# Padding the narrow fp32 matmuls of a recurrent layer to the whole array, and an earlier place for its spreads

## The reference

```python
xx = jnp.pad(h, ((0, 0), (1, 0), (0, 0)))[:, :T] - h
xr, xw, xk, xv, xa, xg = (h + xx * mu[i] for i in range(6))
r = xr @ w_r
k = xk @ w_k
v = xv @ w_v
logw = -jax.nn.softplus(-(w0 + jnp.tanh(xw @ w1) @ w2)) - 0.5
a = jax.nn.sigmoid(a0 + (xa @ a1) @ a2)
g = jax.nn.sigmoid(xg @ g1) @ g2
kk = (k * k_k).astype(jnp.float32).reshape(B, T, H, N)
kk = kk / jnp.maximum(jnp.sqrt(jnp.sum(kk * kk, axis=-1, keepdims=True)), 1e-12)
k = k * (1.0 + (a - 1.0) * k_a)
...
m = jnp.mean(y, axis=-1, keepdims=True)
var = jnp.mean(jnp.square(y - m), axis=-1, keepdims=True)
y = ((y - m) * lax.rsqrt(var + GN_EPS)).reshape(B, T, D) * ln_g + ln_b
bonus = (jnp.sum(rh * kh * r_k, axis=-1, keepdims=True) * vh).reshape(B, T, D)
out = ((y + bonus) * g).astype(h.dtype) @ w_o
```

## Time and profile before

| | us |
|---|---|
| median of 3 runs | 2586.24 (2584.41 to 2588.34) |
| span of the profiled execution | 2583.7 |
| PE busy | 2498.8 (97%), 12240 instructions |
| DVE busy | 1161.4 (45%) |
| ACT busy | 937.5 (36%) |
| POOL busy | 1020.1 (39%) |
| mean granted clock of PE | 0.982 of full |

### The profile page before, as it was taken

How to read it: one execution, slowest core, us unless ns; L and a number is a source line. 1 busy time by engine, 2 the same in 40 slices (tenths; PEclk the granted TensorE clock), 3 DMA queues, 4 the chain that set the end, 5 groups by cost and what they waited for, 6 DMA issues and landing times.

```text
span 2583.7 us, 32306 instructions
## 1 busy us (share of the span) xinstructions
PE 2498.8 (97%) x12240; PEld 1938.1 (75%) x12240; DVE 1161.4 (45%) x1979; ACT 937.5 (36%) x1582; POOL 1020.1 (39%) x617
## 2 busy tenths in 40 slices
PE   7999999999989999999999999999999899999998
PEld 5776567888846668885787888888767687888887
DVE  5113654113152676643723365164389533562462
ACT  3545553222245462223443422123333534322222
POOL 4331545444522232212561545345424443445344
PEclk9999899999989999898999999999999999999999
DMA  3122013333411110002331233233222221333232
GB/s 129 58 66 87 17 33 89 95 96 96 126 49 49 57 58 2 2 1 77 110 117 50 82 98 107 89 97 98 82 66 85 87 90 58 90 97 108 88 94 69
DMA packets 55567, 196.99 MB, mean 76 GB/s; under 512 B 6701, under 2 KB 8877, under 8 KB 54733
## 3 DMA queue, kind: packets, MB, share of 16 engines
q1 hardware_dynamic: 54464, 192.44, 24.2%
q10 hardware_dynamic: 974, 2.80, 0.3%
HBM read 193.12 MB, written 2.10 MB: 76 GB/s over the span
## 4 chain that ended last, share of the span: by engine, by line
PE 46%; DVE 6%; ACT 1%; issue 0%; DVEq 0%; ACTq 0%
PE ps L364 11%; PE ps L366 11%; PE ps L365 11%; DVE ps L2993 4%; PE ps L439 3%; PE ps L440 3%; PE ps L441 3%; PE ps L2836 1%; PE ps L2859 1%; PE ps L3006 1%; DVE ps L3155 0%; PE ps L2604 0%; PE ps L2636 0%; PE ps L2609 0%; PE ps L2846 0%; PE ps L3050 0%
## 5 line engine op out<-in xcount | busy, mean ns | idle before, releaser
L463 POOL TENSOR_TENSOR w_lo<-raw,w_hi 128x1024 fp32r<-128x1024 f32 x342 | 819.6, 2407 | 1015.4 <-ACT w_hi L455 1015.1
L364 PE MATMUL ps<-ahead_hi,w_hi 128*128 128x512 f32 x1216 | 481.0, 396 | 2.0 <-issue 2.0
L366 PE MATMUL ps<-ahead_hi,w_lo 128*128 128x512 f32 x1216 | 473.3, 389 | 0.0
L365 PE MATMUL ps<-ahead_lo,w_hi 128*128 128x512 f32 x1216 | 473.1, 389 | 0.0
L455 ACT ACTIVATE w_hi<-raw 128x1024 fp32r<-128x1024 f32 x342 | 352.8, 1049 | 172.1 <-PE ps L441 91.1
L364 PEld LDWEIGHTS ps<-ahead_hi,w_hi 128*128 128x128 f32 x1216 | 228.3, 188 | 53.0 <-issue 6.4
L365 PEld LDWEIGHTS ps<-ahead_lo,w_hi 128*128 128x128 f32 x1216 | 228.3, 188 | 50.8 <-issue 4.1
L730 DVE TENSOR_TENSOR x_stream<-x_stream,ps 128x512 f32<-128x512 f32 x79 | 54.3, 688 | 468.4 <-PE ps L366 278.4
L366 PEld LDWEIGHTS ps<-ahead_hi,w_lo 128*128 128x128 f32 x1216 | 228.3, 188 | 47.8
L3127 ACT ACTIVATE ffn_s<-ps 128x512 f32<-128x512 f32 x44 | 26.4, 599 | 322.3 <-DVE ps L3155 322.3
L439 PE MATMUL ps<-ffn_a_hi,w_hi 128*128 128x512 f32 x342 | 133.5, 390 | 3.0 <-DVE ffn_a_lo L3160 2.9
(11 more groups left out here) (431 smaller groups left out, 4625.2 us busy)
## 6 DMA issues: line engine op xcount, KB each, us to landing
raw<-in_wall SPq DMA_DIRECT2D x346, 512.0 KB, 3.6
x_stream<-in_x SPq DMA_DIRECT2D x8, 256.0 KB, 7.5
cw<-in_cmp_w SPq DMA_DIRECT2D x1, 2048.0 KB, 7.9
out_y<-x_stream SPq DMA_DIRECT2D x16, 128.0 KB, 1.8
lora_a<-in_lora_a ACTq DMA_DIRECT2D x1, 1152.0 KB
dist<-in_consts SPq DMA_DIRECT2D x1, 1088.0 KB, 11.0
mem<-in_mem SPq DMA_DIRECT2D x1, 1024.0 KB, 5.9
gwb<-in_lora_b SPq DMA_DIRECT2D x1, 1024.0 KB
```

The lines of the kernel that those rows point to most:

```text
L364: pe.matmul(out, hi, src.hi[:, t, 0:width], start=first, stop=False)
L365: pe.matmul(out, hi, src.lo[:, t, 0:width], start=False, stop=False)
L366: return pe.matmul(out, lo, src.hi[:, t, 0:width], start=False, stop=last)
L463: e.tensor_tensor(self.w.lo[:, s, :], self.raw[:, s, :], as_float(self.w.hi[:, s, :]), ALU.subtract).then_inc(lo_r.sem, 1)
```

## The change

All of these matmuls get an operand of more than 64 rows or columns:

- `WIDE` is 66. Head sums, bonus sums and the variance take a slice of 66 columns from the constants (`k.own(m)`) in place of 16 columns of `picks`, and their result has 66 rows, of which the upper 50 are zero sums. The spreads (L1870, L2401, L2636) contract 66 rows; the added rows of the spread matrix are zero. ACT and DVE treat 66 rows where they treated 16 (roots, maximum, reciprocal, the copy of the bonus). `picks` and its transfer are gone from the recurrent layer.
- The low-rank inputs take all 128 columns from their first column on; the last part of the gate, 32 columns, now starts at column 160 and lands in rows 96 to 127. The rate matmul and the second gate matmul contract 128 rows; DVE clears the rows that they add, with two memsets, and ACT waits for these too.
- Transfers: `lora_b` 128 rows for 65, the spread matrix 66 rows for 16 (twice), the constants two columns more.

And the places: `middle` is called behind every step. The queries' spread of tile t-1 is issued behind step 1 of tile t, `cumulate(1)` stays behind step 3; spread(7) is issued behind step 1 of the values' tile 0. On DVE `key_normed` comes ahead of `bonus_in`.

```diff
--- before.py
+++ after.py
@@ -52,5 +52,6 @@
 HEAD_TILES = 10
-
-
-CONST_SIZES = [("ident", 128), ("blockones", 128), ("negtri", 128), ("m4", 512), ("cum", 129), ("own", 2 * HEAD_TILES - 2 + 64),
+WIDE = 66
+
+
+CONST_SIZES = [("ident", 128), ("blockones", 128), ("negtri", 128), ("m4", 512), ("cum", 129), ("own", 2 * HEAD_TILES - 2 + WIDE),
                ("fan_scale", 1), ("fan_bias", 1),
@@ -148,2 +149,7 @@
         return self.vecs[:, c:c + 1]
+
+    def own(self, m):
+
+        c = CST["own"] + 2 * HEAD_TILES - 2 - 2 * m
+        return self.consts[:, c:c + WIDE]
 
@@ -414,4 +420,4 @@
                             mm.then_inc(self.released.sem, 1)
-                        if self.middle is not None and q == 3:
-                            self.middle(pe, 4 * i + j)
+                        if self.middle is not None:
+                            self.middle(pe, 4 * i + j, q)
                     mm.then_inc(used.sem, 1)
@@ -1594,3 +1600,3 @@
 
-    PARTS = ((1, 5, 0, 64), (4, 6, 64, 64), (5, 7, 128, P), (5, 4, 256, 32))
+    PARTS = ((1, 5, 0), (4, 6, 64), (5, 7, 128), (5, 4, 160))
 
@@ -1613,3 +1619,3 @@
         pe.matmul(k.ps[:, 4, :], k.ones[:, :], k.squares[:, :], start=True, stop=True).then_inc(summed.sem, 1)
-        rec.wait(pe, "lora_loaded", 64)
+        rec.wait(pe, "lora_loaded", 48)
         for m in range(KD):
@@ -1618,5 +1624,5 @@
                 rec.wait(pe, "lora_mixed", t + 1)
-                for mu, bank, c, w in self.PARTS:
+                for mu, bank, c in self.PARTS:
                     if mu == i:
-                        mm = pe.matmul(k.ps[0:w, bank, :], rec.lora_a[:, m, c:c + w], rec.mixes[:, t % 6, :], start=(m == 0),
+                        mm = pe.matmul(k.ps[:, bank, :], rec.lora_a[:, m, c:c + P], rec.mixes[:, t % 6, :], start=(m == 0),
                                        stop=(m == KD - 1))
@@ -1629,3 +1635,3 @@
         act.activation(k.root[:, :], k.ps[:, 4, :], ACT.Sqrt, scale=1.0 / D, bias=k.bias[1e-6]).then_inc(root.sem, 1)
-        rec.wait(act, "constant_made", 3)
+        rec.wait(act, "constant_made", 5)
         for m in range(KD):
@@ -1645,3 +1651,3 @@
         rec.done(act.activation(rec.inner_g[:, 0, :], k.ps[:, 7, :], ACT.Sigmoid), "lora_inner")
-        rec.done(act.activation(rec.inner_g[0:32, 1, :], k.ps[0:32, 4, :], ACT.Sigmoid), "lora_inner")
+        rec.done(act.activation(rec.inner_g[96:P, 1, :], k.ps[96:P, 4, :], ACT.Sigmoid), "lora_inner")
 
@@ -1654,2 +1660,4 @@
         rec.done(v.memset(rec.inner_w[64:65, :], 1.0), "constant_made")
+        rec.done(v.memset(rec.inner_a[64:P, :], 0.0), "constant_made")
+        rec.done(v.memset(rec.inner_g[0:96, 1, :], 0.0), "constant_made")
         v.wait_ge(root.sem, root(1))
@@ -1697,3 +1705,2 @@
         self.sm, self.omka, self.keeps = s.tile("sm", KD, 12), s.tile("one_minus_ka", KD), s.tile("one_minus_mu", 48)
-        self.picks = s.tile("picks", 4 * HEAD_TILES - 2)
         s = at(151)
@@ -1731,3 +1738,3 @@
             "state_zeroed", "y_sums", "y_taken", "spread_loaded")}
-        k.advance(64, "lora_loaded")
+        k.advance(48, "lora_loaded")
         k.advance(KD, "spread")
@@ -1753,5 +1760,4 @@
 
-        for dst, src in ((self.lora_a[:, :, :], self.a["lora_a"]), (self.wb[0:65, :, :], self.a["lora_b"][0:65, 0:2, :]),
-                         (self.picks[:, :], self.a["consts"][:, CST["pick"]:CST["spread"]]),
-                         (self.spread[0:2 * KD, :], self.a["consts"][0:2 * KD, CST["spread"]:CST["spread"] + D])):
+        for dst, src in ((self.lora_a[:, :, :], self.a["lora_a"]), (self.wb[:, :, :], self.a["lora_b"][:, 0:2, :]),
+                         (self.spread[0:WIDE, :], self.a["consts"][0:WIDE, CST["spread"]:CST["spread"] + D])):
             self.done(e.dma_start(dst, src), "lora_loaded", 16)
@@ -1780,3 +1786,3 @@
         sp.wait_ge(self.v_used.sem, self.v_used(KD))
-        self.done(sp.dma_start(self.wide[0:2 * KD, :], self.a["consts"][0:2 * KD, CST["spread"]:CST["spread"] + D]),
+        self.done(sp.dma_start(self.wide[0:WIDE, :], self.a["consts"][0:WIDE, CST["spread"]:CST["spread"] + D]),
                   "spread_loaded", 16)
@@ -1808,5 +1814,4 @@
     def heads_sum(self, pe, m):
-        c = HEAD_TILES * 2 - 2 - 2 * m
         pe.wait_ge(self.k_free.sem, self.k_free(m + 1 + RING))
-        self.done(pe.matmul(self.k.ps[0:2 * KD, 7, :], self.picks[:, c:c + 2 * KD], self.sq[:, m % 2, :], start=(m == 0),
+        self.done(pe.matmul(self.k.ps[0:WIDE, 7, :], self.k.own(m), self.sq[:, m % 2, :], start=(m == 0),
                             stop=(m == KD - 1)), "heads_summed")
@@ -1819,3 +1824,3 @@
             wait(pe, "rates", t)
-        done(pe.matmul(k.ps[:, 4, :], self.wb[0:64, 1, t * P:(t + 1) * P], self.inner_a[0:64, :], start=True, stop=True),
+        done(pe.matmul(k.ps[:, 4, :], self.wb[:, 1, t * P:(t + 1) * P], self.inner_a[:, :], start=True, stop=True),
              "rate_sums")
@@ -1869,3 +1874,3 @@
             self.wait(pe, "kk_inverse", 2)
-        self.done(pe.matmul(self.k.ps[:, 6, :], self.spread[0:2 * KD, self.chunk(p)], self.rt[0:2 * KD, :], start=True,
+        self.done(pe.matmul(self.k.ps[:, 6, :], self.spread[0:WIDE, self.chunk(p)], self.rt[0:WIDE, :], start=True,
                             stop=True), "spread")
@@ -1874,12 +1879,11 @@
 
-        c = HEAD_TILES * 2 - 2 - 2 * p
         self.wait(pe, "bonus_in", p + 1)
-        self.done(pe.matmul(self.k.ps[0:2 * KD, 7, :], self.picks[:, c:c + 2 * KD], self.t0[:, :], start=(p == 0),
+        self.done(pe.matmul(self.k.ps[0:WIDE, 7, :], self.k.own(p), self.t0[:, :], start=(p == 0),
                             stop=(p == KD - 1)), "bonus_sums")
 
-    def queries_middle(self, pe, t):
-        if t == 1:
+    def queries_middle(self, pe, t, q):
+        if t and q == 1:
+            self.spread_tensor(pe, t - 1)
+        if t == 1 and q == 3:
             self.cumulate(pe, 1)
-        if t:
-            self.spread_tensor(pe, t - 1)
 
@@ -1919,3 +1923,3 @@
         k, wait, done = self.k, self.wait, self.done
-        t, rows = 4 * i + j, 2 * KD
+        t, rows = 4 * i + j, WIDE
         if t == 0:
@@ -1964,2 +1968,4 @@
         wait(v, "key_gained", p + 1)
+        wait(v, "spread", p + 1)
+        done(v.scalar_tensor_tensor(A_, A_, k.vec("k_k", p), k.ps[:, 6, :], ALU.mult, ALU.mult), "key_normed")
         if p:
@@ -1967,4 +1973,2 @@
         done(v.scalar_tensor_tensor(self.t0[:, :], r, k.vec("r_k", p), K_, ALU.mult, ALU.mult), "bonus_in")
-        wait(v, "spread", p + 1)
-        done(v.scalar_tensor_tensor(A_, A_, k.vec("k_k", p), k.ps[:, 6, :], ALU.mult, ALU.mult), "key_normed")
         wait(v, "grown", 2 * p + 2)
@@ -1979,5 +1983,7 @@
 
-    def values_middle(self, pe, t):
-        if t == 1:
+    def values_middle(self, pe, t, q):
+        if t == 0 and q == 1:
             self.spread_tensor(pe, KD - 1)
+        if q != 3:
+            return
         for p in ((), (2,), (), (5,), (7,), (), (), ())[t]:
@@ -2039,3 +2045,3 @@
                 wait(act, "bonus_sums", KD)
-                done(act.activation(self.bonus[0:2 * KD, :], k.ps[0:2 * KD, 7, :], ACT.Copy), "bonus_kept")
+                done(act.activation(self.bonus[0:WIDE, :], k.ps[0:WIDE, 7, :], ACT.Copy), "bonus_kept")
             self.gather(act, p)
@@ -2400,3 +2406,3 @@
         wait(pe, "spread_loaded", 16)
-        done(pe.matmul(k.ps[:, 3, :], self.wide[0:2 * KD, self.chunk(p)], self.bonus[0:2 * KD, :], start=True, stop=True),
+        done(pe.matmul(k.ps[:, 3, :], self.wide[0:WIDE, self.chunk(p)], self.bonus[0:WIDE, :], start=True, stop=True),
              "spread_sums")
@@ -2590,3 +2596,3 @@
         pe.matmul(k.ps[:, 5 + m % 3, :], self.wb[:, 0, m * P:(m + 1) * P], self.inner[:, 0, :], start=True, stop=False)
-        pe.matmul(k.ps[:, 5 + m % 3, :], self.wb[0:32, 1, m * P:(m + 1) * P], self.inner[0:32, 1, :], start=False, stop=True
+        pe.matmul(k.ps[:, 5 + m % 3, :], self.wb[:, 1, m * P:(m + 1) * P], self.inner[:, 1, :], start=False, stop=True
                   ).then_inc(go.sem, 1)
@@ -2594,3 +2600,3 @@
     def tensor(self, pe):
-        k, y, rows = self.k, self.y, 2 * KD
+        k, y, rows = self.k, self.y, WIDE
         me, ce, sq, va, rt, iv, sp_r, go, n1, n2, nd, zh, zl = self.marks
@@ -2607,4 +2613,3 @@
             pe.wait_ge(sq.sem, sq(m + 1))
-            c = CST["own"] + HEAD_TILES * 2 - 2 - 2 * m
-            pe.matmul(k.ps[0:rows, 2, :], k.consts[:, c:c + rows], self.sqt[:, m % 2, :], start=(m == 0),
+            pe.matmul(k.ps[0:rows, 2, :], k.own(m), self.sqt[:, m % 2, :], start=(m == 0),
                       stop=(m == KD - 1)).then_inc(va.sem, 1)
@@ -2625,3 +2630,3 @@
 
-        k, rows = self.k, 2 * KD
+        k, rows = self.k, WIDE
         iv, sp_r, n1 = self.marks[5], self.marks[6], self.marks[8]
@@ -3357,3 +3362,3 @@
     lora_b[0, 64] = n["rwkv_w0_2"][0]
-    lora_b[2], lora_b[3, :32] = n["rwkv_g2_2"][0][:P], n["rwkv_g2_2"][0][P:]
```

(3 more changed lines are left out.)

## The result

| | before | changed |
|---|---|---|
| median of 4 runs, us | 2585.32 (2576.16 to 2588.34) | 2568.09 (2565.78 to 2569.46) |
| ratio, 95% interval | | 0.9942 (0.9922 to 0.9962) |
| span of the profiled execution | 2583.7 | 2567.7 |
| mean granted clock of PE | 0.982 | 0.984 |
| PE busy | 2498.8 | 2474.2 |

The medians differ by 17 us (the ratio, which is taken run against run, says 10 to 20), the profiled spans by 16.0; 4 were forecast, and 2577.5 was the low end. The kernel is faster, by a way that the forecast had at nothing.

The account below looks back on a forecast made before the run. TensorE was taken as the bound in the keys and memory stages, DVE in the queries; -8.1 + 3.3 + 2.6 + 3.4 - 2.4 - 2.7 = -3.9 us took the median 2586.24 to 2582.3, range 2577.5 to 2586.0.

Parts of the forecast that it names:

- State loop: State loop: late spreads stand among 64 by 64 products, so a change of shape stays on both sides: 0.
- the rule that the prediction used: TensorE's clock falls back after idle gaps between matmul bursts; a sum without the rule would be 3.4 lower.
- The price of a fall: On the path: a slow stretch lasts 3.5 us at half clock, so one fall costs 1.7; two taken, +3.4.
- Cost of the moves: Queries' tile 1 loses 3.3 us, values' tiles 0 and 1 lose 2.6, two clock falls add 3.4.
- Inputs and keys: Low-rank inputs -3.5 us and keys -5.2: TensorE enters the queries 8.7 earlier, the first reciprocal comes 8.1 earlier.
- Queries' loop: Queries, tiles 2 to 7: DVE paces them, so padding only lengthens TensorE's wait and the early spread costs nothing: 0.
- GroupNorm: GroupNorm: TensorE's variance and mean pair shrinks from 2.02 to 1.72 us; -2.4 at the start of the memory stage.
- Memory stage: Second block's memory stage: gate and spread save a little under 0.39 us per tile over eight tiles; 2.7 kept.
- C: Rival, whole kernel: padding saves nothing and only the moves act, +10 us, 2596.3; chance 0.05.
- A: Rival, new stalls: one fall of the clock (-5.6 us, 2580.6) or none (-7.3, 2578.9); chance 0.33.
- B: Rival, queries and values: the moves help and neither stall costs, -13 us, 2573; chance 0.07.
- End of the program: Stretch behind the memory stage up to the program's end: no further shift forecast, 0.

Follow-up runs that it names:

- e7: All of the padding with spreads and DVE operations in their old places, but late spreads contract 64 rows instead of 66: 2558.6 us, ratio 0.9906.
- e3: All of the padding without the moves, spreads and the two DVE operations in their old places: 2553.9 us, ratio 0.9878 against the kernel before.
- e1: The changed kernel with only the state loop's late spreads put back to contracting 16 rows: 2579.2 us, ratio 0.9977 against the kernel before.
- e2: The kernel before with only the late spreads padded to 66 rows, and the bonus sums to 66 columns: 2571.3 us, ratio 0.9945.
- e6: The changed kernel with only the last spread put back in the values' tile 1, fourth step: 2560.2 us, ratio 0.9908 against the kernel before.
- e4: The kernel before with the new places and new DVE order alone, no padding: 2591.1 us, ratio 1.0022.
- e10: All padding, early spreads and new DVE order; first spread behind cumulate(1), last at the values' tile 1, second step: 2555.3 us, ratio 0.9895.
- e9: All of the padding with spreads and DVE operations in their old places, but late spreads contract 32 rows: 2557.1 us, ratio 0.9898.

## Why the prediction was wrong

- **State loop: 0. This is the step that failed.** It measured -14.3. The term was held at nothing for two reasons, and both fell. The products behind the late spread are of 64 by 64 in the first tile only; in the others the padding saves 0.19 each (1.4 up to the last tile, e7 against e3). And above all, the low clock of that stretch, 0.93 before, was taken as given. The falls there have no idle time in front of them, so the rule that the prediction used, falls behind stalls, did not see them. The Trainium skill, "TensorE: Matmul & The Clock Gate", "Why this matters for your kernels", advises against idle gaps between bursts. At the two stalls of the changed kernel these traces agree; that avoiding gaps is not enough to keep the clock up, the loop of the kernel before shows. The forecast missed by 13 us; e1 gives 11 of them back with eight narrow matmuls, and e2 has 9.6 in the loop from eight wide ones.
- **The price of a fall, 1.7, was too low as well.** It is half of a stretch of 3.4, but the stretches behind the two stalls were 6.8 long. The earlier trace rows had one of 13.6 behind a stall beside the one of 3.5 that was taken. How long it is differs between executions with the same stall: behind the first one, of 3.52 to 3.54, it was 6.8 in the changed kernel and 3.4 in e1 and e6, and behind the stall of 2.21 in e4 there was none. From the reciprocal to the queries' loop DVE lost 6.2, 5.0, 4.9 and 3.5 us in these four. The idle times themselves were right to half a microsecond.
- **Cost of the moves, 9.3 (3.3 + 2.6 + 3.4):** 14 by the medians, 13.2 at the start of the solve (e3). Up to the queries' loop the forecast of -3.1 and the measured -2.8 agree by luck, since two errors cancel: without the stall it is -9.6 (e3, from the end of the first block) where the prediction had -8.1, and the stall with its falls cost 6.9 where it had 5.0. In the values the move cost 6.3 where it had 4.3, and the solve came at +3.3 against the first block's end, where +1.2 was forecast. (The terms of the start of products(1) add up to 933.2 and not to 933.4, which changes nothing.)
- **Inputs and keys, -8.7:** right. The reciprocal, forecast at -8.1, starts 8.0 earlier, 9.0 against the first block's end. About 1 of it comes from the slow stretch in the low-rank inputs, 10.2 long where it was 13.7 before: in e6, where it is 13.7 again, the reciprocal is 7.8 earlier.
- **Queries' loop, 0:** right (e10).
- **GroupNorm, -2.4:** -0.8. The slow stretch of 10.2 (1201.6 before, 1193.1 after) reaches 1.6 us further into GroupNorm, since that starts 10 earlier and the stretch only 8.5. In e1, where it reaches as far as before, the gain is 1.6. So the stretch is half of the miss; the other half is open.
- **Memory stage, -2.7:** -2.95, right.
- **Rivals.** C, padding without effect, is out: in e3 the solve starts 9.9 earlier against the first block's end, and the whole is 31 us faster than before. The same page's "K=32 single mm = same time as K=128" holds for the matmul's own time (1.12 at 16 rows, 1.13 at 66), not for its neighbours, which start later at 16 rows, nor for the clock. C's other half, the moves alone, was priced at +10 and measured +5.9 (e4; 7.7 at the start of the solve in its profiled execution, which was its slowest). A and B named too little and for wrong reasons. None had the clock inside the state loop.
- **End of the program, 0:** -2.0, where slow stretches of 13.6 us before are 10.2 after. The change is not the cause: e7 and e9, with all of the padding, have 13.6 there and gain 0.1.

So the change joins three things: a gain on the path from shape (13.8 priced; about 14 measured, with the 1 us of the inputs' stretch in it), a gain of about 13 from the clock in the state loop, not priced, and a loss of 14 from two moves, priced at 9.3.
